# Attention output parts summed in the output stage, and the negated maxima in one instruction

## The reference

```python
s = jnp.einsum('bqhd,bkhd->bhqk', q, k, preferred_element_type=jnp.float32) * scale
p = jax.nn.softmax(s, axis=-1)
o_mix = jnp.einsum('bhqk,bkhd->bqhd', p.astype(v.dtype), v)      # 12 heads of 64
...
o = jnp.concatenate([o_mix, o_mem], axis=-1) * jax.nn.silu(gate)
x = x + o @ w_out[i]
```

## Time and profile before

| | |
|---|---|
| median of 3 runs | 3508.45 us (3508.15 to 3511.12) |
| profiled execution | 3507.9 us, its span 3505.9 us |
| mean granted TensorE clock | 0.968 of full speed |
| busy, share of the span | PE 94%, PEld 79%, DVE 57%, ACT 48%, POOL 40% |

### The profile page before, as it was taken

How to read it: one execution, slowest core, us unless ns; L and a number is a source line. 1 busy time by engine, 2 the same in 40 slices (tenths; PEclk the granted TensorE clock), 3 DMA queues, 4 the chain that set the end, 5 groups by cost and what they waited for, 6 DMA issues and landing times. The chain is left out here.

```text
span 3505.9 us, 47874 instructions
## 1 busy us (share of the span) xinstructions
PE 3293.0 (94%) x17708; PEld 2785.0 (79%) x17708; DVE 2003.7 (57%) x2897; ACT 1685.7 (48%) x2412; POOL 1391.6 (40%) x914
## 2 busy tenths in 40 slices
PE   8969969999999999999799996996999979999899
PEld 8968847777777777777589996885888869999787
DVE  4447768888888888888543333443333343333432
ACT  4446637777777777777644443102222234444200
POOL 1148748888888888888600000000000010000000
PEclk9979979999999999999999998998999979999999
DMA  7768882323232122321233225884222253222565
GB/s 282 258 238 312 309 245 49 66 64 67 64 67 49 45 62 63 68 62 26 108 133 107 85 88 164 223 231 181 89 91 96 101 194 130 91 87 83 154 194 160
DMA packets 380211, 454.50 MB, mean 130 GB/s; under 512 B 51704, under 2 KB 317304, under 8 KB 367728
## 3 DMA queue, kind: packets, MB, share of 16 engines
q1 hardware_dynamic: 380016, 451.91, 41.8%
HBM read 262.07 MB, written 189.64 MB: 129 GB/s over the span
## 5 line engine op out<-in xcount | busy, mean ns | idle before, releaser
L1254 POOL TENSOR_TENSOR at_acc<-at_acc,at_ph 128x1024 f32<-128x1024 f32 x288 | 690.8, 2398 | 76.8 <-ACT at_ph L1180 55.9
L1180 ACT ACTIVATE at_ph<-at_sc 128x1024 fp32r<-128x1024 f32 x408 | 418.6, 1026 | 321.6 <-PE at_sc L1100 321.2
L1288 DVE TENSOR_TENSOR at_pl<-at_sc,at_ph 128x1024 fp32r<-128x1024 f32 x408 | 498.5, 1222 | 129.6 <-ACT at_sc L1181 129.4
L1274 DVE TENSOR_REDUCE at_mx<-at_mxp 128x1 f32<-128x512 f32 x816 | 522.1, 681 | 24.8 <-PE at_mxp L1111 24.0
L1181 ACT ACTIVATE at_sc<-at_sc 128x1024 f32<-128x1024 f32 x408 | 415.6, 1019 | 0.0
L171 PE MATMUL gm_gate<-gm_h,gm_g_hi 128*128 128x256 f32 x1280 | 366.9, 287 | 0.0
L172 PE MATMUL gm_gate<-gm_h,gm_g_hi 128*128 128x256 f32 x1280 | 362.1, 283 | 0.0
L173 PE MATMUL gm_gate<-gm_h,gm_g_lo 128*128 128x256 f32 x1280 | 361.9, 283 | 0.0
L1096 PE MATMUL at_sc<-at_qt,at_kt 97*128 97x512 f32 x816 | 330.5, 405 | 4.1 <-DVE at_pl L1288 2.1
L1098 PE MATMUL at_sc<-at_qt,at_kt 96*128 96x512 f32 x816 | 324.8, 398 | 0.0
L1125 PE MATMUL at_o_hi<-at_ph,at_v 128*128 128x512 f32 x816 | 322.5, 395 | 2.1 <-DVE at_half L1293 2.1
(11 more groups left out here) (245 smaller groups left out, 7363.7 us busy)
## 6 DMA issues: line engine op xcount, KB each, us to landing
gm_h<-hT SPq DMA_DIRECT2D x48, 1024.0 KB, 6.9
hT<-lat_n_h SPq DMA_DIRECT2D x24, 1024.0 KB, 6.1
hT<-sg_n_h SPq DMA_DIRECT2D x24, 1024.0 KB, 3.8
qT<-hd_stq SPq DMA_DIRECT2D x60, 384.0 KB, 5.1
kT<-hd_stk SPq DMA_DIRECT2D x60, 384.0 KB, 4.5
at_qt<-qT SPq DMA_DIRECT2D x120, 192.0 KB, 3.0
sgT<-gm_sg SPq DMA_DIRECT2D x80, 256.0 KB, 2.1
ou_o<-omix SPq DMA_DIRECT2D x40, 512.0 KB, 6.4
```

Source lines behind the costliest of these rows:

```text
L1180: act.activation(ph[:, g], sc[g % 2][:], ACT.Exp, scale=SCALE).then_inc(p_hi, 1)
L1254: pool.tensor_tensor(acc[:, c.slot, :], f32(ph[:, (g - 1) % 4]).rearrange("p b n -> p (b n)") if t == 1 else acc[:, c.slot, :], now, ALU.a ...
L1274: dve.tensor_reduce(mx[:, n:n + 1], mxp[n % 2][:], AX.X, ALU.max).then_inc(mx_in, 1)
L1288: dve.tensor_tensor(pl[:, g], sc[g % 2][:], f32(ph[:, g]), ALU.subtract).then_inc(p_lo, 1)
```

## The change

The values' low part, rows 0 to 63 of `o_hi`, is no longer added in attention. ACT copies it to a new tile `rest`, between its copies to `up` and `low`; SP stores `rest` to a second scratch, `omix_low` (128 KB a chunk), and POOL adds `up` and `low` for `omix`. DVE's `halves` is gone. TensorE's first values wait for `rest` and `low`; ACT's copy to `up` now waits for POOL's `join` of the chunk before. In layer 0's output stage SP loads a tile of `omix_low` too (384 KB, 128 rows x 6 pieces of 512 bytes) and DVE adds it to `o` ahead of the multiplication by the reciprocals. Of the maxima, one `tensor_reduce` with `negate=True` writes `neg`; `m4` is gone and `mx` has two halves.

```diff
--- before.py
+++ after.py
@@ -946,11 +946,10 @@
         tot = s.sb("tot", [P, 2, BLK])
         tot_hi = s.sb("tot_hi", [P, 2, BLK], F32R)
         tot_lo = s.sb("tot_lo", [P, 2, BLK], F32R)
-        mx = s.sb("mx", [P, 16])
-        m4 = s.sb("m4", [P, 4])
+        mx = s.sb("mx", [P, 2, 16])
         neg = s.sb("neg", [P, 2, 4], F32R)
         up = s.sb("up", [VH, BLK])
-        half = s.sb("half", [VH, BLK])
+        rest = s.sb("rest", [VH, 2, BLK])
         low = s.sb("low", [ROW_HI + 1, 2, BLK])
         ost = s.sb("ost", [VH, 2, BLK])
...
@@ -986,7 +984,7 @@
 
         def stored(c):
 
-            return c.half * 48 - (16 if c.slot == 0 else 0)
+            return c.half * 64 - (16 if c.slot == 0 else 0)
...
@@ -1033,11 +1031,14 @@
                     return sums_out[which, c.head:c.head + 1, c.part * BLK:(c.part + 1) * BLK]
 
                 def store(c):
+                    sp.wait_ge(rest_in, c.n + 1)
                     sp.wait_ge(low_in, c.n + 1)
                     sp.dma_start(sum_rows(c, 1), low[ROW_LO:ROW_LO + 1, c.slot, :]).then_inc(o_out[c.slot], 16)
                     if has_before(c):
                         sp.dma_start(sum_rows(before(c, 1), 0),
                                      low[ROW_HI:ROW_HI + 1, c.slot, :]).then_inc(o_out[c.slot], 16)
+                    sp.dma_start(omix_low[c.head * VH:(c.head + 1) * VH, c.part * BLK:(c.part + 1) * BLK],
+                                 rest[:, c.slot, :]).then_inc(o_out[c.slot], 16)
                     sp.wait_ge(o_in, c.n + 1)
                     dst = omix[c.head * VH:(c.head + 1) * VH, c.part * BLK:(c.part + 1) * BLK]
                     sp.dma_start(dst, ost[:, c.slot, :]).then_inc(o_out[c.slot], 16)
...
@@ -1115,7 +1116,7 @@
                 def value(c, t):
                     if t == 0:
                         pe.wait_ge(v_load[c.kv], loaded(c))
-                        after(pe, half_in, c.n)
+                        after(pe, rest_in, c.n)
                         after(pe, low_in, c.n)
                     g = (c.g0 + t) % 4
...
@@ -1185,11 +1186,11 @@
 
                 def upper(c):
                     act.wait_ge(valued, c.g0 + c.pairs)
-                    after(act, half_in, c.n)
+                    after(act, o_in, c.n)
                     act.copy(up[:], o_hi[VH:2 * VH, :]).then_inc(up_in, 1)
                     if c.n >= 2:
                         act.wait_ge(o_out[c.slot], stored(c))
-                        act.wait_ge(o_in, c.n - 1)
+                    act.copy(rest[:, c.slot, :], o_hi[0:VH, :]).then_inc(rest_in, 1)
                     act.copy(low[:, c.slot, :], o_lo[0:ROW_HI + 1, :]).then_inc(low_in, 1)
...
@@ -1231,11 +1231,11 @@
                                        ALU.subtract).then_inc(tot_lo_in, 1)
 
                 def join(c):
-                    pool.wait_ge(half_in, c.n + 1)
+                    pool.wait_ge(up_in, c.n + 1)
                     pool.wait_ge(low_in, c.n + 1)
                     if c.n >= 2:
                         pool.wait_ge(o_out[c.slot], stored(c))
-                    pool.tensor_tensor(ost[:, c.slot, :], half[:], low[0:VH, c.slot, :],
+                    pool.tensor_tensor(ost[:, c.slot, :], up[:], low[0:VH, c.slot, :],
                                        ALU.add).then_inc(o_in, 1)
...
@@ -1271,26 +1271,21 @@
                 def maxima(c, pieces):
                     for n in pieces:
                         dve.wait_ge(mx_mm, c.mx0 + (n + 1))
-                        dve.tensor_reduce(mx[:, n:n + 1], mxp[n % 2][:], AX.X, ALU.max).then_inc(mx_in, 1)
+                        if n == 0:
+                            after(dve, neg_in, c.n - 1)
+                        dve.tensor_reduce(mx[:, c.slot, n:n + 1], mxp[n % 2][:], AX.X, ALU.max).then_inc(mx_in, 1)
                     if len(pieces) and pieces[-1] == c.pieces - 1:
                         dve.wait_ge(mx_in, c.mx0 + c.pieces)
-                        dve.tensor_reduce(m4[:], mx[:, 0:c.pieces].rearrange("p (q n) -> p q n", q=4),
-                                          AX.X, ALU.max).then_inc(m4_in, 1)
-                        dve.wait_ge(m4_in, c.n + 1)
                         if c.n >= 2:
                             dve.wait_ge(row_in[c.slot], c.half * 64)
-                        dve.tensor_scalar(neg[:, c.slot, :], m4[:], -1.0, None, ALU.mult).then_inc(neg_in, 1)
+                        dve.tensor_reduce(neg[:, c.slot, :], mx[:, c.slot, 0:c.pieces].rearrange("p (q n) -> p q n", q=4),
...
-
-                def halves(c):
-                    dve.wait_ge(up_in, c.n + 1)
-                    after(dve, o_in, c.n)
-                    dve.tensor_tensor(half[:], o_hi[0:VH, :], up[:], ALU.add).then_inc(half_in, 1)
 
...
@@ -1303,12 +1298,9 @@
                 def step(c):
                     for t in range(c.pairs):
                         low_of(c, t)
-                        if has_before(c) and t == 1:
-                            halves(before(c, 1))
                         maxima(*max_pieces(c, t))
 
                 run_chunks(dve, step)
-                halves(Chunk(Chunk.COUNT - 1))
...
@@ -1808,17 +1800,18 @@
         o = s.sb("o", [P, 2, KD, P])
         sg = s.sb("sg", [P, 2, KD, P])
         r = s.sb("r", [P, 2, DIV, P]) if inv_s is not None else None
+        o2 = s.sb("o2", [P, 2, DIV, P]) if inv_s is not None else None
...
         y_out = [s.sem(f"y_out{u}") for u in range(2)]
-        LOADS = 64 if inv_s is not None else 32
+        LOADS = 80 if inv_s is not None else 32
...
@@ -1828,6 +1821,7 @@
                     sp.dma_start(o[:, u], omix[:, ts].rearrange("(k p) t -> p k t", p=P)).then_inc(o_in[u], 16)
                     sp.dma_start(sg[:, u], sgT[:, ts].rearrange("(k p) t -> p k t", p=P)).then_inc(o_in[u], 16)
                     if inv_s is not None:
+                        sp.dma_start(o2[:, u], omix_low[:, ts].rearrange("(k p) t -> p k t", p=P)).then_inc(o_in[u], 16)
                         for n in range(2):
...
@@ -1885,6 +1879,8 @@
                     u = i % 2
                     dve.wait_ge(o_in[u], LOADS * (i // 2 + 1))
                     if inv_s is not None:
+                        dve.tensor_tensor(o[:, u, 0:DIV], o[:, u, 0:DIV], o2[:, u], ALU.add).then_inc(added, 1)
+                        dve.wait_ge(added, i + 1)
                         dve.tensor_tensor(o[:, u, 0:DIV], o[:, u, 0:DIV], r[:, u], ALU.mult
                                           ).then_inc(divided, 1)
                         dve.wait_ge(divided, i + 1)
...
@@ -2117,6 +2113,7 @@
     kT = scratch("kT", [TILES, 3, P, 2, 3, P])
     vS = scratch("vS", [TOK, NH * 2 * VH])
     omix = scratch("omix", [D, TOK])
+    omix_low = scratch("omix_low", [NH * VH, TOK])
...
             gated_output(nc, K, *next(steps), omix, sgT, lambda i, src=src: tile_of(src, i),
-                         lambda i, dst=dst: tile_of(dst, i), f"ou{layer}", inv_s if layer == 0 else None)
+                         lambda i, dst=dst: tile_of(dst, i), f"ou{layer}", *((inv_s, omix_low) if layer == 0 else ()))
```

More of the change, by code:

```diff
@@ L929, in max_pieces, with attention @@
     return ahead, [at - ahead.mx0, at - ahead.mx0 + 1] if ahead.exists() else []
-def attention(nc, K, qT, kT, vS, omix, sums_out):
+def attention(nc, K, qT, kT, vS, omix, omix_low, sums_out):
     SCALE = float(QK) ** -0.5
@@ L960, in attention @@
         (const_in, scored, p_hi, p_in, p_lo, summed, folded, tot_hi_in, tot_lo_in, tot_mm,
-         valued, mx_mm, mx_in, m4_in, neg_in, up_in, low_in, half_in, o_in) = (s.sem(n) for n in (
+         valued, mx_mm, mx_in, neg_in, up_in, rest_in, low_in, o_in) = (s.sem(n) for n in (
              "const", "scored", "p_hi", "p_in", "p_lo", "summed", "folded", "tot_hi_in",
-             "tot_lo_in", "tot_mm", "valued", "mx_mm", "mx_in", "m4", "neg", "up_in", "low_in", "half_in",
-             "o_in"))
+             "tot_lo_in", "tot_mm", "valued", "mx_mm", "mx_in", "neg", "up_in", "rest_in", "low_in", "o_in"))
         q_load = [s.sem(f"q_load{u}") for u in range(4)]
@@ L1081, in _ @@
                 for u in range(2):
-                    n = 48 * (Chunk.COUNT) // 2 - (16 if u == 0 else 0)
+                    n = 64 * (Chunk.COUNT) // 2 - (16 if u == 0 else 0)
                     sp.wait_ge(o_out[u], n + (16 if u != last.slot else 0))
@@ L1213, in _ @@
                 act.wait_ge(tot_mm, last.n + 1)
-                act.wait_ge(o_out[1 - last.slot], stored(last) + (16 if last.slot == 0 else 0)
-                            - (16 if last.slot == 1 else 0) + (48 if last.slot == 1 else 0))
+                act.wait_ge(o_out[1 - last.slot], (last.half + 1) * 64 - 16)
                 act.copy(low[ROW_HI:ROW_HI + 1, 1 - last.slot, :], o_lo[ROW_HI:ROW_HI + 1, :]
@@ L1273, in maxima @@
                         dve.wait_ge(mx_mm, c.mx0 + (n + 1))
-                        dve.tensor_reduce(mx[:, n:n + 1], mxp[n % 2][:], AX.X, ALU.max).then_inc(mx_in, 1)
+                        if n == 0:
```

(16 more changed lines are left out.)

## The result

The changed kernel takes 3522.7 us (median of 7 runs, 3520.7 to 3525.0); the kernel before took 3508.45 beside it. The ratio is 1.0039, with a 95% interval of 1.0027 to 1.0051: slower by 14.3 us, as forecast in sign and inside the range, but only two thirds of the 22 us forecast. The profiled execution after took 3524.4 us.

The account below looks back on a forecast made before the run. TensorE was taken as the bound in attention and, once running, in the first output stage. Terms 14.1 - 0.7 + 0.5 + 7.1 + 1.0 = 22.0 us on 3507.9 gave 3529.9, stated as 3530 us, range 3516 to 3546.

Parts of the forecast that it names:

- The third copy: ScalarE at 47 boundaries into prompt chunks: exponential 0.30 us later after 0.20 to 0.30 of cover (idle, overlap); +14.1 us.
- What VectorE is spared: Attention: without `halves` and `neg`, VectorE mostly idles for ScalarE's exponential instead; -0.7 us, bounds 0 and -1.4.
- Waits and stores in attention: TensorE's first values, ScalarE's wait for POOL's join and SP's 60 more stores in attention: no cost.
- The output stage's start: First output stage: new load and sum delay tile 2 by 3d + 2.0, d being the load's DMA time; +7.1 us.
- Rate of the output stage: Later output-stage tiles: DMA time per tile against TensorE's 10.88 us, partly absorbed by the tiles' lead; +1.0 us, bounds 0 and 4.
- the d that I took: Output stage: time of all DMA engines for the new 384 KB load, taken as 1.7 us between 1.35 and 2.06.
- the end of attention: At attention's very end one more copy stands in the last chain; +0.5 us.
- my main case: Whole kernel: the forecast's own case, ScalarE's copy and the output stage's start both paid; 3522 to 3540 us, chance 0.58.
- the cheap one: Rival: load hidden except 2.4 us at the first tile, copy 8.9 us; 3518.5, case 3515 to 3522, chance 0.12.
- The full DMA queue as a bound: Rival: the DMA queue becomes the output stage's bound, 17 us there instead of 8.1; 3539 to 3548 us, chance 0.20.
- No change: Rival: ScalarE's copy takes up slack everywhere, only the output stage's start costs; 3510 us, chance 0.05.
- faster: Rival: VectorE sets the pace, and sparing it `neg` removes the 0.35 us end-of-chunk wait; 3494 us, chance 0.05.

Follow-up runs that it names:

- e4: The changed kernel without ScalarE's copy to `rest`, the second scratch being stored from `low` instead; 3512.6 us, ratio 1.0012.
- e6: The changed kernel with the copy of rows 0 to 63 made twice on ScalarE, once to an unread tile; 3549.1 us, ratio 1.0115.
- e5: The changed kernel without the 60 stores of `rest`, the output stage loading the first scratch twice; 3519.3 us, ratio 1.0031.
- e11: The changed kernel without the 60 stores, measured again beside a repeat of the changed kernel; 3520.3 us, ratio 1.0036.
- e9: The changed kernel without the load of `omix_low`, VectorE's added sum kept but over the gate's tile; 3515.3 us, ratio 1.0021.
- the second measurement: The changed kernel itself measured once more against the kernel before; 3521.3 us, ratio 1.0038.
- e1: The kernel before with only the new negated maxima from one `tensor_reduce`; 3506.0 us, ratio 0.9992.
- e8: The kernel before with the new maxima and the next chunk's first scores ahead of the last pair of maxima; 3490.4 us, ratio 0.9951.

## Why the prediction was right, and where its size was off

- **The third copy, 14.1 forecast: the mis-sized term.** The mechanism was as forecast (e4: without the copy the wait is gone; e6: with another it grows by the copy's full spacing). The failed step is "Left are 0.19 to 0.41 us ... I take the middle, 0.30". The exponential came 0.17 later and TensorE's gap grew by 0.16 where I took 0.30. Over the 47 boundaries that made 7.3 us (20.6 to 27.9), since the 11 into a next head grew by about 0.1 only, and by its lengths of attention e4 gives 8.2 to 9.5. My lower bound was 8.9. I had priced the copy between 0.49 and 0.61. The 0.61 belongs to the copy right behind `up`, which was there before; the copy that was added takes 0.48, and all 0.30 of the cover counted. Here the sentence of the Trainium skill that I did not stake the sum on (ScalarE: Activation LUTs, What ACT_TABLE_LOAD costs: back-to-back ACTIVATEs overlap by about 93 ns) was the better guide. The rows of the added copy agree with it, 0.58 long and 0.48 apart, and it gave 8.9. Behind `up` it does not hold: that distance is 0.60 to 0.62 us in all 60 chunks, before and after, and why stays open. That I counted the boundary from prompt to sample chunk only once was right for one copy; with two it costs some 4 us more (e6).
- **What VectorE is spared, -0.7 forecast: about -1.7.** Of some 60 us of work taken away, 1.7 came back (before against e4), for the reason given: `pl` waits for ScalarE. That is 0.3 beyond my bound, but traces of one and the same attention differ by as much as 1.6, so it cannot be told from the 0.7. The waits in the window fell at the maxima, from 21.9 to 18.1 us.
- **Waits and stores in attention, 0: right** (e5, e11). The first values did not stall.
- **The output stage's start, +7.1: right in sum, wrong in make-up.** Tile 2 came 6.8 us later, but tile 0 2.0 and tile 1 5.8 where the steps said 2.7 and 5.4. The sum alone is free (e9) where I counted 1.0 at each of tiles 0 and 1 in full; the load alone costs 3.5, near the 3 x 1.35 = 4.05 of the price by bytes and under the 5.1 that I took; together they cost what I said. By these traces the parts by themselves came to less than I counted, and an effect between them that I did not foresee made up for it: that the sum was right is luck.
- **Rate of the output stage, +1.0: it was 0.2** (7.0 less 6.8). The share rose by 0.16 of 10.88 us, 1.7 us a tile, which is the d that I took, and at that d my own working gave nothing beyond the tiles' lead; the 1.0 was an allowance for a larger one.
- **Sum.** In this pair of traces attention is 6.5 us longer (8.2 - 1.7 by e4), the output stage 7.0, and the end of attention 0.3, where I had 0.5: 13.8, against 14.3 by the medians. The spans differ by 16.5, of which 2.4 are the spread before the gates.
- **Where the time fell.** 3522.7 is at the very edge between my main case (3522 to 3540) and the cheap one (3515 to 3522), and the second measurement, 3521.3, lies in the latter. The mechanism tells them apart, not the time: TensorE did wait for the first three tiles, 6.8 us more by tile 2, where the cheap case had 2.4.
- **The rivals.** The full DMA queue as a bound: the share came, the cost did not. The cheap case was near in the copy's price (8.9) and wrong in the load's (2.4 for 7.0). No change and faster: out, the latter by e1. The end-of-chunk gap, which that rival laid to VectorE, goes when TensorE's order is changed (e8) and stays when VectorE is spared work (e1, e4).
- **A reading.** "0.23 from 900.29 to the next" in the prediction is a slip: the next start is 900.72, and the 0.23 is the distance from the matmul before. Nothing in the sum hangs on it.

The Trainium skill (SBUF — State Buffer, Who interferes with whom) says that on this chip a `tensor_reduce` never contends with GpSimd. The trace agrees: the new one takes 0.16 to 0.17 us in all 60 chunks, where the `tensor_scalar` took from 0.17 to 1.68. That the 30 us thus spared bought next to nothing (e1) says what a wait on an engine with slack is worth.

## What to carry to other kernels

Work added to an engine that is busy 75% of the time may cost more than work taken from one at 88% gives back: read which of them the bound engine's wait ends on, at the place, and price the addition by its distance to the next start (0.48) less the idle time ahead of the releaser (0.20) and the overlap (0.10). Where a reduction with two buffers follows its matmuls, put other matmuls that are ready ahead of the pair that has to wait for a free buffer: here it saved about 15 us of attention, more than the whole change cost and more than moving the copy to VectorE gave back (8 us). If a copy has to be made, make it on the engine that waits.

## What the hardware showed that I had not expected

- DMA engines at a busy share of 1.01 over 120 us, 266 GB/s, did not slow the tiles that they feed once the first three were in: 531 matmuls in those 120 us, as with 0.85. From tile 3 on VectorE's waits for loads rose from 9.3 us to 32.9 (over the whole stage from 38.3 to 66.0) without reaching TensorE. A share of 1 alone doesn't tell that the queue is the bound.
- The load of 384 KB cost 3.5 to 4 us by itself at the stage's start, about 3 x 1.3. VectorE's 1.0 us sum cost nothing without it and, by one trace, some 3 us with it.
- The same stretch of the same code, from the first matmul behind attention's stage to the first gates from the loaded tiles, took 36.5 to 39.0 us in fourteen traces. One pair of traces can't tell 2 us of a whole program. Single distances are far steadier: those before the scores of unit 4 add up to 27.9 to 28.1 us in eight traces.
